# An earlier wait in the filled PE stream, a reordered DVE tail, and the four head pairs as a loop

## The reference, cut to what matters

```python
def gated_deltanet_mixer(h, w_in, conv_w, a_log, dt_bias, o_gain, w_out):
    proj = h @ w_in
    qkv, z, ab = jnp.split(proj, [A_CONV_CH, A_CONV_CH + A_V_W], axis=-1)
    qkv = jax.nn.silu(causal_depthwise_conv(qkv, conv_w))          # 4 taps
    ...
    o = chunk_gated_delta_rule(q, k, v, g, beta)                   # per head, over chunks of tokens
    o = rms_norm(o, o_gain) * jax.nn.silu(z)
    return o.reshape(B, T, A_V_W) @ w_out
```

## Time and profile before

| | |
|---|---|
| device time, median of 3 runs | 2802.29 us (2801.84 to 2807.29) |
| the profiled execution: its time, its span | 2807.29 us, 2805.7 us |
| PE busy | 2685.5 us, 96% of the span |
| DVE, ACT, POOL busy | 1625.6 us, 1000.8 us, 375.6 us |
| mean granted TensorE clock | 0.970 |
| second pair, from its first square sums (L808) to the next pair's | 216.0 to 342.8 us of the span |
| last pair | from 469.7 us; it ends before 532 us |

### The profile page before, as it was taken

How to read it: one execution, slowest core, us unless ns; L and a number is a source line. 1 busy time by engine, 2 the same in 40 slices (tenths; PEclk the granted TensorE clock), 3 DMA queues, 4 the chain that set the end, 5 groups by cost and what they waited for, 6 DMA issues and landing times.

```text
span 2805.7 us, 37635 instructions
## 1 busy us (share of the span) xinstructions
PE 2685.5 (96%) x14601; PEld 2179.1 (78%) x14601; DVE 1625.6 (58%) x2360; ACT 1000.8 (36%) x1412; POOL 375.6 (13%) x275
## 2 busy tenths in 40 slices
PE   7999999889999979999999999999999987999997
PEld 5788887766777768888888888888887775888886
DVE  6665657555666665444634455544446897644455
ACT  4544536345556542222342222422223212422222
POOL 1100001002000011111221111211110440211110
PEclk9999999989999989999989999999999996999998
DMA  3222312112222212322213223232222210223221
GB/s 112 91 75 62 105 47 90 32 60 83 75 82 75 70 51 90 104 90 98 82 61 102 93 90 104 90 104 91 97 97 75 71 49 15 88 92 103 91 90 59
DMA packets 167797, 227.27 MB, mean 81 GB/s; under 512 B 5361, under 2 KB 148219, under 8 KB 167699
## 3 DMA queue, kind: packets, MB, share of 16 engines
q1 hardware_dynamic: 163523, 217.23, 23.6%
q0 software_dynamic: 2368, 8.47, 0.9%
q10 hardware_dynamic: 1808, 0.21, 0.1%
HBM read 223.71 MB, written 2.18 MB: 81 GB/s over the span
## 4 chain that ended last, share of the span: by engine, by line
PE 83%; DVE 9%; issue 4%; ACT 3%; DMA 0%; POOL 0%; DVEq 0%; ACTq 0%; SPq 0%; POOLq 0%
PE ps L376 20%; PE ps L377 20%; PE ps L378 20%; PE ps L760 4%; PE ps L762 3%; PE ps L761 3%; DVE w_lo L357 2%; DVE dw_y L2074 1%; DVE probs L1595 1%; PE ps L1465 1%; PE ps L366 1%; PE ps L367 1%; PE ps L368 1%; PE ps L1476 1%; PE ps L1447 1%
## 5 line engine op out<-in xcount | busy, mean ns | idle before, releaser
L352 ACT ACTIVATE w_hi<-w_raw 128x2048 fp32r<-128x2048 f32 x203 | 388.4, 1913 | 912.1 <-PE ps L378 902.5
L376 PE MATMUL ps<-h_hi,w_hi 128*128 128x512 f32 x1472 | 574.4, 390 | 4.2 <-DVE glu L2043 3.6
L378 PE MATMUL ps<-h_hi,w_lo 128*128 128x512 f32 x1472 | 573.5, 390 | 0.0
L377 PE MATMUL ps<-h_lo,w_hi 128*128 128x512 f32 x1472 | 573.2, 389 | 0.0
L357 DVE TENSOR_TENSOR w_lo<-w_raw,w_hi 128x2048 fp32r<-128x2048 f32 x203 | 471.5, 2323 | 122.7 <-ACT w_hi L352 122.7
L421 DVE SCALAR_TENSOR_TENSOR xT<-ps,xT 128x512 f32<-128x512 f32 x504 | 336.6, 687 | 151.0 <-PE ps L378 149.7
L376 PE MATMUL ps<-a_hi,w_hi 128*128 128x512 f32 x1024 | 402.6, 393 | 20.0 <-issue 15.2
L377 PE MATMUL ps<-a_lo,w_hi 128*128 128x512 f32 x1024 | 401.1, 392 | 0.0
L378 PE MATMUL ps<-a_hi,w_lo 128*128 128x512 f32 x1024 | 400.8, 391 | 0.0
L1679 POOL TENSOR_TENSOR f_gate<-f_gate,n_rstd 128x512 f32<-128x512 f32 x88 | 176.8, 2011 | 1123.2 <-ACT f_gate L1673 1123.2
L376 PEld LDWEIGHTS ps<-h_hi,w_hi 128*128 128x128 f32 x1472 | 276.7, 188 | 62.8 <-DVE glu L2043 4.5
(11 more groups left out here) (334 smaller groups left out, 3036.3 us busy)
## 6 DMA issues: line engine op xcount, KB each, us to landing
w_raw<-in_ffn_w_in_dram SPq DMA_DIRECT2D x88, 1024.0 KB, 5.1
w_raw<-in_ffn_w_out_dram SPq DMA_DIRECT2D x44, 1024.0 KB, 4.9
w_raw<-in_a_w_in_dram SPq DMA_DIRECT2D x24, 1024.0 KB, 5.5
w_raw<-in_b_w_in_dram SPq DMA_DIRECT2D x16, 1024.0 KB, 5.4
w_raw<-in_conv_w_pw_dram SPq DMA_DIRECT2D x12, 1024.0 KB, 5.6
w_raw<-in_a_w_out_dram SPq DMA_DIRECT2D x8, 1024.0 KB, 4.9
w_raw<-in_b_w_out_dram SPq DMA_DIRECT2D x8, 1024.0 KB, 4.9
bias_cur<-rel_scratch POOLq DMA_DIRECT2D x8, 512.0 KB, 3.9
```

The costliest lines, as they stand in the source:

```text
L352: nc.scalar.activation(w_hi[:, t % 2], w_raw[:, t % 2], ACT.Copy).then_inc(hi_done, 1)
L376: nc.tensor.matmul(dst, wh, xh, start=(k == 0), stop=False)
L377: nc.tensor.matmul(dst, wh, xl, start=False, stop=False)
L378: m = nc.tensor.matmul(dst, wl, xh, start=False, stop=last)
```

## The change

- In the solve, PE's filler is cut in two: `ahead` goes from 3 to 2, and a new `over()` issues one step behind the wait. In the last pair `ahead` stays 1 and `over()` issues nothing. The `fill` calls of the chunk scan write `ahead` in place of the same numbers. The number and order of PE's matmuls stay the same; twelve waits stand one step earlier.
- In the tail on DVE, the order was: add 4, tap 0, add 5, tap 1, adds 6 and 7, tap 2, adds 0 and 1 of tile t + 1, tap 3, adds 2 and 3, split of the next pair's first tile, adds 4 to 7. It becomes: add 4, tap 0, add 5, tap 1, add 6, tap 2, add 7, tap 3, split, adds 0 to 7 of tile t + 1. In the last pair the order stays.
- On all five engines, the first three pairs become a loop (`Fori(0, 3)`); the last is written out behind it.

```diff
@@ -826,6 +826,10 @@
 
             combos = [(4 * a + c, a, c) for a in heads for c in range(TC)]
 
+            def over():
+
+                fill(0 if last_pair(i) else 1)
+
             def turn_values(d):
                 for a in heads:
                     a_dve.wait(pe, f"vb{d - 1}{a}" if d else f"kd{a}", i)
@@ -834,10 +838,11 @@
                         ins = tr(pb(2 + a, c), v(qkv, 4 + d + 2 * a, c), ident[:])
                     a_pe.done(f"vt{a}{d}", ins)
 
-            ahead = 1 if last_pair(i) else 3
+            ahead = 1 if last_pair(i) else 2
             for l in lv:
                 fill(ahead)
                 a_dve.wait(pe, f"T{l - 1}", i)
+                over()
                 for k, a, c in combos:
                     for n, r in enumerate(ROWS):
                         ins = mm(small_block(ps[r, 4], k), lower_T[r, a, c * P + n * BK:c * P + n * BK + BK],
@@ -902,7 +912,7 @@
                     if c:
                         ins = mm(b, v(neg_wT, a, c), state[:, a], start=False, stop=True)
                     a_pe.done(f"vn{c}{a}", ins)
-                fill(1 if last_pair(i) else 2)
+                fill(ahead)
                 for a in heads:
                     a_act.wait(pe, f"vn{c}{a}", i)
                     if c == 0:
...
@@ -1259,21 +1269,13 @@
             t, r, period = a_tile_at(6, i)
             add_chunks(dve, t, range(0, 4), r, period)
             split(7)
-            if last:
-                add_chunks(dve, t, range(4, 8), r, period)
-                add_chunks(dve, t + 1, range(0, 8), r, period, stat=1)
-                return
-            add_chunks(dve, t, (4,), r, period)
-            dve_tap(dve, 6, 0, i)
-            add_chunks(dve, t, (5,), r, period)
-            dve_tap(dve, 6, 1, i)
-            add_chunks(dve, t, (6, 7), r, period)
-            dve_tap(dve, 6, 2, i)
-            add_chunks(dve, t + 1, (0, 1), r, period)
-            dve_tap(dve, 6, 3, i)
-            add_chunks(dve, t + 1, (2, 3), r, period)
-            split_tile(dve, 4 + NA, i, NA)
-            add_chunks(dve, t + 1, range(4, 8), r, period)
+            for n in range(4):
+                add_chunks(dve, t, (4 + n,), r, period)
+                if not last:
+                    dve_tap(dve, 6, n, i)
+            if not last:
+                split_tile(dve, 4 + NA, i, NA)
+            add_chunks(dve, t + 1, range(0, 8), r, period, stat=1 if last else None)
...
@@ -2533,8 +2538,9 @@
             dve_a_first(dve)
             gates_dve.wait(dve, "be")
             gates_act.wait(dve, "last")
-            for i in range(A_PAIRS):
+            with dve.Fori(0, A_PAIRS - 1) as i:
                 dve_a(dve, i)
+            dve_a(dve, A_PAIRS - 1)
             dve_rstd(dve, 1, copied=True)
             dve_h(dve, 1, 1, gain_of("kv_norm"))
             kv_dve.begin(dve)
@@ -2567,8 +2573,9 @@
             a_pe.begin(pe)
             pe.wait_ge(setup_const, SETUP_CONSTS)
             pe_a_first(pe)
-            for i in range(A_PAIRS):
+            with pe.Fori(0, A_PAIRS - 1) as i:
                 pe_a(pe, i)
+            pe_a(pe, A_PAIRS - 1)
             pe_stat(pe, 1, T_KV)
             kv_pe.begin(pe)
             pe_kv(pe)
```

More of the change, by code:

```diff
@@ L2396, in a_loads @@
                     load(sp, t, rows256(a_w_out[0], bass.ds(i * 512 + 256 * k, 256)), r, period)
-            for i in range(A_PAIRS):
+            with sp.Fori(0, A_PAIRS - 1) as i:
                 a_loads(i)
+            a_loads(A_PAIRS - 1)
             for k in range(2):
@@ L2449, in _ @@
             a_gp.begin(pool)
-            for i in range(A_PAIRS):
+            with pool.Fori(0, A_PAIRS - 1) as i:
                 gp_a(pool, i)
+            gp_a(pool, A_PAIRS - 1)
             pool.wait_ge(rel_stored, 16)
@@ L2489, in _ @@
             act.wait_ge(rel_stored, 16)
-            for i in range(A_PAIRS):
+            with act.Fori(0, A_PAIRS - 1) as i:
                 act_a(act, i)
+            act_a(act, A_PAIRS - 1)
             act_squares(act, 1, added(T_A_END - 1))
```

## The result

The change makes the kernel slower: median 2823.02 us (2812.67 to 2825.64, 8 runs) against 2802.80 us (2801.84 to 2807.91, 8 runs), a ratio of 1.0068 with a 95% interval of 1.0051 to 1.0086. The forecast was 2813, in a range up to 2821. The sign was right, and the time lies 10 us above the forecast and 2 us above its range.

The account below looks back on a forecast made before the run. PE, busy in 96% of the span, was taken to bound the kernel. Terms 7.1 (tail) + 3.4 (clock) + 0 (earlier wait) + 0.4 (loop) = 10.9 us on a median of 2802.3 gave 2813 us, range 2804 to 2821.

Parts of the forecast that it names:

- The tail: DVE's reordered tail: add 0 of tile t + 1 comes late, PE stalls once per tail, 3 x 2.37 = 7.1 us.
- The clock behind the tail stalls: Half clock for 3.4 us, losing 1.7 us, behind two of three tail stalls: 3.4 us, ends 0 and 5.1.
- The earlier wait: Solve: DVE's result needed 0.68 us earlier is still covered, and the 0.32 us step stays: 0 us.
- The loop: Loop on all engines: register work is covered, each jump costs between nothing and 1.7 us; 0.4 us taken.
- a cover of 3.8 us: At the jump back, PE's sequencer runs ahead while PE still computes until about 215.4: 3.8 us.
- Its upper bound: Jumps back: with a 1 MB weight load's 5.5 us as slowest nearby, up to 1.7 us each, two 3.4 us.
- The harmless tail: Rival: DVE reaches the split with time to spare, no stall or clock drop, 0.4 us left, 2802.7; chance 0.12.
- the vanishing gap of the solve: Rival: gap before the solve's small products goes with the wait; 2800.6 at full 0.35 us, 2810.0 at 0.09; chance 0.08.
- The fetching jump: Rival: both jumps back fetch code at 1.7 us each, plus one more clock drop of 1.7: 2817.9; chance 0.14.
- L376 for L421 three times at 2.1 us: Sign in PE's waits: O tile waits for DVE's add, a new row, three times, about 2.1 us each.
- half clock behind two of the stalls: Sign on PE: a clock of 0.50 for some us behind two of the tail stalls.
- no gap over 0.3 us at the jumps: Sign on PE at the loop's two jumps back: no gap over 0.3 us.

Follow-up runs that it names:

- e2: Kernel before with only the new DVE tail order, pairs written out flat: 2817.58 us, ratio 1.0048.
- e6: The whole change, but PE's four pairs written out flat: 2813.66 us, ratio 1.0034 against the kernel before.
- g1: The whole change, with the weight load that falls on PE's jump held until DVE has split the next tile: 2821.31 us, ratio 1.0059 against the kernel before.
- h1: The whole change with 30 small products ahead of the first pair, shifting PE's code by 120 instructions: ratio 1.0048 against the kernel before.
- e1: Kernel before with only the solve's waits one filler step earlier, flat, old tail: 2802.95 us, ratio 1.0000.
- e5: Kernel before with the earlier waits and a loop on PE alone, old tail: 2809.24 us, ratio 1.0023.
- e8: Kernel before with earlier waits and PE's loop over the first two pairs only, the others flat: 2803.75 us, ratio 1.0005.
- e10: Shortened pair (some 1700 PE instructions, work left out), earlier waits, PE loop over three pairs: 2802.80 us, against 2799.84 for the same flat; one run each.
- f1: Kernel before with earlier waits, flat, plus 34 small products in front, shifting PE's code by 136 instructions: ratio 1.0019.
- f2: Kernel before with earlier waits and PE's loop, plus 30 small products in front, shifting PE's code by 120 instructions: ratio 1.0016.
- h2: Kernel before with earlier waits, flat, plus 64 small products in front, shifting PE's code by 256 instructions: ratio 1.0028.
- e3: The change without the new tail (earlier waits and all five loops): 2808.94 us, ratio 1.0018 against the kernel before.

## Why the forecast was wrong in size

**The tail (7.1 us): right in mechanism, place and size.** Three stalls, one per tail, 2.1 us each as the profile counts, 7.1 us in periods. e2 shows them without the loop.

**The clock behind the tail stalls (3.4 us): mechanism right, too dear in the profiled executions.** It was taken at two stalls of three, from two cases in another stage. After, e2, e6, g1 and h1 have fifteen such stalls with four drops, one each in after, e2, e6 and h1, none in g1. Each drop of 3.4 us cost 1.6 to 1.8, so the term was 1.7 in after. What decides which of these equal stalls is followed by a drop stays open.

**The earlier wait (0): right.** e1 gives a ratio of 1.0000, and the step of 0.32 us is where it was.

**The loop (0.4 us): the first step that failed.** "So a jump costs between nothing and 1.7 us, two of them up to 3.4 us; I take 0.4, as the small packet is the nearer row." The two jumps cost 4.2 us, plus 1.7 for a clock drop right behind the first. That the body doesn't stay was allowed for. What was mis-sized is the price. It was taken as the length of a packet (1.1 us) against a cover of 3.8 us. The branch itself takes 3.3 to 4.8 us when the fetch has the DMA engines nearly for itself, which just eats the cover (e5, e8), and 4.0 to 6.3 us when a weight load is under way (h1, after). The packet is the smaller part of it: at e5's first jump it starts 1.0 us behind the branch's start, takes 1.3, and the branch ends another 1.4 later. The two edits that were costed apart meet here: the new tail puts the load ahead of the jump. The forecast had this in hand, as it noted that the split comes 2.4 us earlier, but it asked only whether PE waits for the split and not what the split releases. Its upper bound took the load's 5.5 us as the whole wait. After's first jump waited 2.1 us behind the load and took 4.2 more, and its 2.9 us lost lie beyond that bound.

The forecast set the Trainium skill's page "Runtime: NRT & Kernel Launch", section "Instruction fetch mechanics", beside this: a taken branch to code that isn't resident must fetch first. The trace agrees, at 3.3 to 6.3 us a branch. It doesn't agree on how much stays. That page of the Trainium skill gives TensorE's instruction memory 2048 instructions, and yet e10's body of some 1700 was fetched anew at each jump. It also lets a jump go without a fetch only inside the current window of two pages, by estimate 512 instructions from its blocks of 256, and the attention loop's 1020 stayed. Here the measurements decide.

**What had no term: the last pair, the second step that failed.** The forecast took it out of the account because its order of work is not changed. It lost 7.7 us, more than the tail: 2.0 us idle in the dense small products, with no engine waited for, and 5.8 us at half clock behind it. f1, f2, h1 and h2 show that this is the place of the code. It can't be called part of the loop's own cost, as f1 pays it without any loop and f2 has the loop without it. Added up, the loop was 3.8 us short with 1.7 for its clock drop, the last pair 7.7 short and the tail's clock 1.7 too dear: 10.9 + 3.8 + 1.7 + 7.7 - 1.7 = 22.4 us, the distance of the two profiled executions.

**The rivals.** The harmless tail and the vanishing gap of the solve are out (e2, e1). The fetching jump was the nearest, at 0.14 and 2817.9; it had the right place but not the last pair. Without the last pair's 7.7 us the profiled execution stands at 14.8 us above before, near that rival's 15.6, by a somewhat different sum.

By the signs that the forecast named: L376 for L421 three times at 2.1 us, yes; eight adds behind the split, yes; solve steps at 0.32 us, yes; half clock behind two of the stalls, behind one; no gap over 0.3 us at the jumps, no (2.7 and 1.2 us), with the fetch packets that speak for code that doesn't stay.

## What to carry to other kernels

Cost a long loop body at the time of the branch, not of a packet: the branches took 3.3 to 4.8 us here, up to 6.3 where a large transfer was under way, and PE idles for what the work queued behind its sequencer doesn't cover. Two edits that are each cheap can meet at one place, so walk the timeline of the whole change, queue by queue. And an edit that changes the number of instructions shifts all code behind it: where products are small and dense, look there for idle time put down to issue, and try a shift by some 120 instructions before blaming the edit.

## What the runs showed of the hardware that was not expected

- Idle time that comes and goes with the place of the code. Between the 24th or 25th and the next of 64 products of 32 columns PE stood 1.8 to 2.4 us (after, e3, e5, f1, g1) and each time went on 2.2 to 2.4 us after a q8 packet had started. A shift of 120 instructions took it away, one of 136 brought it, one of 256 left all as it was. The packet alone doesn't tell: in every kernel that runs all 64 products one starts within 0.5 us of this group's start. Where PE idled, it came 6.0 to 7.1 us behind the packet before it; elsewhere 3.9 to 4.8.
- A stretch at half clock is 3.4 us long behind the stalls between 512-column matmuls, and 6.8 us (e5, f1, g1) or 13.7 us (after) behind the idle time in the last pair, where PE's work is thin; there it costs 2.6 to 5.8 us. e3 had the same idle time and no drop.
- Executions of one kernel differ: those of before by up to 8 us (2801.2 to 2809.2), those of e3 by 18 (2800.6 to 2818.7). The profiles show one place for some 5 us of it, in the pooling mixer (L1861), some 890 us behind the pairs. Stretch of before, whose profiled execution took 2807.29 us, then the same 51 matmuls in e1, whose profiled span is 2799.7 us:

```profile
1426.00:1439.60 13.60, 13.60 (x51) 12.05 (x52) 6.01 (x7) 4.77 (x7) 6.68 (x4) 0.56 0.02 4
```

```profile
1425.10:1433.10 8.00, 8.00 (x51) 7.16 (x51) 6.37 (x7) 5.30 (x8) 5.42 (x5) 1.00 0.01 2
```

The first is mostly at half clock, the second at full clock, and the work behind the pairs takes 2266.5 and 2261.4 us. All profiled executions have a stretch at half clock in this mixer; those with 2266 to 2268 us behind the pairs have a second one some 20 us later, and those with 2261 to 2263 have not. So a median over few runs can move by some us for a reason that lies far from the change. That is why the periods of the pairs were used wherever the two disagree. They hold for the profiled execution alone: e3's fastest, 2800.6 us, is no slower than the fastest of before, and after's fastest, 2812.7 us, lies only 10 us above before's median, where the idle times of the bill alone make 13.3. So some executions must go without part of the losses shown here, and which part isn't on record.
